# Two eight-product groups ahead of the seven-product bodies, and the up half of the gated unit left unscaled

## What is computed

```python
def rmsnorm(x, gain):
    xf = x.astype(jnp.float32)
    y = xf * lax.rsqrt(jnp.mean(xf * xf, axis=-1, keepdims=True) + EPS)
    return (y * gain.astype(jnp.float32)).astype(x.dtype)

def swiglu_2(x, w1, w3, w2):
    return (jax.nn.silu(x @ w1) * (x @ w3)) @ w2

    h = h + 0.5 * swiglu_2(rmsnorm(h, ffn1_norm[l]), ffn1_w1[l], ffn1_w3[l], ffn1_w2[l])
    ...
    h = h + 0.5 * swiglu_2(rmsnorm(h, ffn2_norm[l]), ffn2_w1[l], ffn2_w3[l], ffn2_w2[l])
```

## Time and profile before

| | |
|---|---|
| median of 3 runs | 1701.44 us (1700.73 to 1702.34) |
| the profiled execution | 1702.09 us |
| its span in the trace | 1700.3 us |
| instructions | 27271 |
| TensorE busy | 1585.5 us, 93% |
| VectorE busy | 1255.2 us, 74% |
| ScalarE busy | 755.0 us, 44% |
| GpSimd busy | 548.5 us, 32% |
| bytes moved | 187.26 MB, 110 GB/s in the mean |

### The profile page before, as it was taken

One profiled execution on the slowest core, in us unless ns is written; L12 is line 12 of the kernel. 1 busy time (PEld: TensorE's weight loads), 2 busy tenths in 40 slices (PEclk: granted clock), 3 DMA queues, 4 the chain that ended last, 5 costly groups with the idle time before them and its releaser, 6 DMA issues. The chain is left out here.

```text
span 1700.3 us, 27271 instructions
## 1 busy us (share of the span) xinstructions
PE 1585.5 (93%) x9945; PEld 1429.7 (84%) x9945; DVE 1255.2 (74%) x1542; ACT 755.0 (44%) x1267; POOL 548.5 (32%) x376
## 2 busy tenths in 40 slices
PE   9999999969999899969898989999998898897998
PEld 7888888859999888759888968888886798897887
DVE  5898665778999645799999874347455999998544
ACT  4553564435555634435545543221231555555322
POOL 0100000285666000175555302152038555551000
PEclk9999999979999999979999989999999899998999
DMA  9535502213343233213323222332212323232232
GB/s 389 202 111 176 188 29 75 75 62 124 123 139 120 71 103 98 101 62 124 123 99 121 77 75 93 118 137 100 75 53 72 122 101 117 100 116 68 91 96 81
DMA packets 34981, 187.26 MB, mean 110 GB/s; under 512 B 3680, under 2 KB 5984, under 8 KB 21472
## 3 DMA queue, kind: packets, MB, share of 16 engines
q1 hardware_dynamic: 30560, 169.53, 28.8%
q0 software_dynamic: 4352, 16.78, 2.8%
HBM read 184.20 MB, written 2.10 MB: 110 GB/s over the span
## 5 line engine op out<-in xcount | busy, mean ns | idle before, releaser
L663 PE MATMUL bank<-t_hi,ring 128*128 128x256 f32 x1920 | 366.5, 286 | 13.5 <-DVE ring L2565 11.2
L663 PE MATMUL bank<-g_hi,w_all 128*128 128x512 f32 (+1 forms) x1088 | 336.3, 391 | 20.3 <-DVE qd L2708 20.3
L2031 DVE TENSOR_TENSOR w_all<-w_raw,w_all 128x2048 fp32r<-128x2048 f32 x80 | 187.1, 2339 | 213.4 <-ACT w_all L1475 213.3
L663 PE MATMUL bank<-a_hi,ring 128*128 128x256 f32 x1440 | 283.1, 289 | 58.5 <-DVE tmp L2634 35.2
L663 PEld LDWEIGHTS bank<-t_hi,ring 128*128 128x128 f32 x1920 | 311.3, 195 | 14.1 <-DVE t_lo L2570 8.3
L663 PEld LDWEIGHTS bank<-a_hi,ring 128*128 128x128 f32 x1440 | 235.0, 195 | 66.9 <-DVE ring L2565 44.0
L1475 ACT ACTIVATE w_all<-w_raw 128x2048 fp32r<-128x2048 f32 x82 | 156.9, 1914 | 282.4 <-PE bank L663 282.4
L663 PE MATMUL bank<-t_lo,ring 128*128 128x256 f32 x960 | 274.6, 286 | 0.0
L663 PEld LDWEIGHTS bank<-g_hi,w_all 128*128 128x128 f32 x1088 | 206.6, 191 | 62.9 <-DVE qd L2708 20.9
L2565 DVE TENSOR_TENSOR ring<-w_sum,ring 128x512 fp32r<-128x512 f32 x240 | 240.8, 1021 | 23.9 <-ACT ring L1767 23.4
L663 PE MATMUL bank<-g_lo,w_all 128*128 128x512 f32 (+1 forms) x544 | 212.2, 390 | 0.0
(11 more groups left out here) (324 smaller groups left out, 2731.1 us busy)
## 6 DMA issues: line engine op xcount, KB each, us to landing
w_raw<-in_ffn_in SPq DMA_DIRECT2D x66, 1024.0 KB, 4.8
w_raw<-in_ffn_out SPq DMA_DIRECT2D x24, 768.0 KB, 4.3
mod_raw<-in_mod POOLq DMA_DIRECT2D x16, 1024.0 KB, 5.5
late<-in_ffn_in SPq DMA_DIRECT2D x30, 512.0 KB, 3.3
w_raw<-in_ffn_out SPq DMA_DIRECT2D x24, 640.0 KB, 3.9
w_raw<-in_gla_in SPq DMA_DIRECT2D x10, 1024.0 KB, 5.1
w_raw<-in_mix_in SPq DMA_DIRECT2D x10, 1024.0 KB, 4.8
mod_w<-in_mod SPq DMA_DIRECT2D x8, 1024.0 KB, 18.7
```

What stands on the lines that cost most here:

```text
L663: return pe.matmul(out, lhs, rhs, start=first, stop=last, skip_group_check=True)
L2031: V.tensor_tensor(flat(w_lo[s]), flat(w_raw[s]), flat(w_hi[s]).bitcast(F32), ALU.subtract).then_inc(lo_done[s], 1)
```

## The change

`BEFORE = 4` hidden chunks are now made by groups, two groups an FFN, and `BODIES` falls from ten to nine. The second group is a plain `group()`: gate unit, then up unit. SyncE loads four units ahead of the bodies' pairs, and `late` waits for four `up_ready`.

In `begin` of both engines the work is put in another order: the second group's two weight splits, the first group's SiLU and hidden chunks, then all four token operands, and only then the ring's first blocks, for they lie over the weights of the second group.

The up chunks are no longer multiplied by the roots. A hidden chunk is silu(gate x roots) x up, and since the roots are one number a token, the output chunks are multiplied by them instead, in PSUM, ahead of their sum (`sum_pair`, `add_half`): eight output chunks an FFN in place of 22 up chunks. Since the up banks are then free once `hid` is written, TensorE waits for `gated` there, not for `up_scaled`.

```diff
+BEFORE = 2 * CPU
+BODIES = (KF - BEFORE) // 2
...
@@ SyncE
-                for s in range(2):
-                    load(s, w_in[s])
+                for n in range(4):
+                    load(n % 2, w_in[n])
...
-                    sp.dma_start(flat(w_raw[s]), w_in[2 + s]).then_inc(pair_loaded[s], 16)
-                sp.wait_ge(up_ready, cnt.next(up_ready, CPU))
-                load_late(w_in[3, :, UNIT // 2:])
+                    sp.dma_start(flat(w_raw[s]), w_in[4 + s]).then_inc(pair_loaded[s], 16)
+                sp.wait_ge(up_ready, cnt.next(up_ready, BEFORE))
+                load_late(w_in[5, :, UNIT // 2:])
@@ TensorE
-                gate_free, up_free = (gate_scaled, up_scaled) if scaled else (silu_done, gated)
+                gate_free, up_free = gate_scaled if scaled else silu_done, gated
...
                 group(True)
+                group()
                 body(True)
@@ ScalarE, begin
+                    if not pair:
+                        split_hi(1)
+                    act.wait_ge(silu_in, cnt.next(silu_in, CPU) if scaled else CPU)
+                    split_hi(0)
+                    if not pair:
+                        copy_roots(5)
+                    gates(0)
+                    act.wait_ge(up_ready, cnt.next(up_ready, CPU))
+                    split_hi(1)
+                    token_upper(0)
+                    token_upper(1)
+                    token_upper(2)
+                    gates(CPU)
...
+                    token_upper(3)
+                    for j in range(4):
                         upper(j, True)
...
@@ VectorE, sum_pair
                     b = bank[banks[c]][:]
+                    if half:
+                        V.tensor_tensor(b, b, roots[:], ALU.mult).then_inc(up_scaled, 1)
+                        dve.wait_ge(up_scaled, cnt.next(up_scaled))
@@ VectorE, begin
+                def ups(m0):
+
+                    for c in range(CPU):
+                        dve.wait_ge(up_ready, cnt.next(up_ready))
+                        dve.wait_ge(silu_done, cnt.next(silu_done))
+                        V.tensor_tensor(hid[:, m0 + c], tmp[c][:], bank[2 + c][:], ALU.mult).then_inc(gated, 1)
+                        cnt.expect(gated)
@@ VectorE, hidden
-                    if scaled:
-                        V.tensor_tensor(tmp[2 + s][:], tmp[2 + s][:], roots[:], ALU.mult).then_inc(up_scaled, 1)
-                        dve.wait_ge(up_scaled, cnt.off(up_scaled, s - 1))
@@ VectorE, add_half
+                out = bank[6 + c][:] if half == 0 else bank[4 + c][:, h]
+                V.tensor_tensor(out, out, roots[:] if half == 0 else roots[:, h], ALU.mult).then_inc(up_scaled, 1)
+                dve.wait_ge(up_scaled, cnt.next(up_scaled))
```

More of the change, by code:

```diff
@@ L1267, in ffn @@
                 cnt.expect(operand_lo, 4)
-                cnt.expect(gate_free, KF - CPU)
-                if not scaled:
-                    cnt.expect(up_free, KF - CPU)
+                cnt.expect(gate_free, KF - BEFORE)
+                cnt.expect(up_free, KF - BEFORE)
                 for j in range(2):
@@ L2575, in hidden_lower, with gates @@
                     V.tensor_tensor(g_lo[:, k], hid[:, k], g_hi[:, k].bitcast(F32), ALU.subtract).then_inc(operand_lo, 1)
+                def gates(first=False):
+                    if not scaled:
+                        cnt.expect(silu_in, CPU)
+                        return
+                    for c in range(CPU):
+                        dve.wait_ge(silu_in, cnt.next(silu_in))
+                        if not first:
+                            dve.wait_ge(gated, cnt.now(gated, 1 - c))
+                        gate = bank[c][:]
+                        if first and pair and c == 0:
+                            dve.wait_ge(dve_step, cnt.now(dve_step))
+                            V.tensor_tensor(tmp[0][:], tmp[0][:], gate, ALU.add).then_inc(dve_step, 1)
+                            dve.wait_ge(dve_step, cnt.next(dve_step))
+                            gate = tmp[0][:]
+                        V.tensor_tensor(tmp[c][:], gate, roots[:], ALU.mult).then_inc(gate_scaled, 1)
+                        cnt.expect(gate_scaled)
+                def ups(m0):
+                    for c in range(CPU):
+                        dve.wait_ge(up_ready, cnt.next(up_ready))
+                        dve.wait_ge(silu_done, cnt.next(silu_done))
+                        V.tensor_tensor(hid[:, m0 + c], tmp[c][:], bank[2 + c][:], ALU.mult).then_inc(gated, 1)
+                        cnt.expect(gated)
                 def begin():
@@ L2586, in begin @@
                             split_lo(1)
-                            x_roots(5, False)
-                        for c in range(CPU):
-                            dve.wait_ge(silu_in, cnt.next(silu_in))
-                            gate = bank[c][:]
-                            if pair and c == 0:
-                                dve.wait_ge(dve_step, cnt.now(dve_step))
-                                V.tensor_tensor(tmp[0][:], tmp[0][:], gate, ALU.add).then_inc(dve_step, 1)
-                                dve.wait_ge(dve_step, cnt.next(dve_step))
-                                gate = tmp[0][:]
-                            V.tensor_tensor(tmp[c][:], gate, roots[:], ALU.mult).then_inc(gate_scaled, 1)
-                            cnt.expect(gate_scaled)
-                    else:
-                        cnt.expect(silu_in, CPU)
+                            x_roots(5)
+                    else:
+                        split_lo(0)
+                    gates(True)
+                    if scaled and pair:
+                        split_lo(0)
+                    ups(0)
+                    split_lo(1)
                     dve.wait_ge(joined, (KD + 2) * n + KD + 1)
                     V.tensor_tensor(t_sum[2][:], a_both[:, QK:KD, TC:T], a_both[:, 0:QK, TC:T], ALU.subtract).then_inc(t_late, 1)
-                    for j in range(3):
-                        lower(j)
                     token_lower(0)
@@ L2608, in begin @@
                     token_lower(1)
[L2609 to L2627 removed]
+                    token_lower(2)
+                    gates()
+                    token_lower(3)
+                    for j in range(4):
+                        lower(j)
+                    ups(CPU)
+                    lower(4)
                 def first_half(s):
```

55 lines of the change are left out of this document (13 added, 42 removed).

## The result

The changed kernel takes 1632.91 us (median of four runs, 1629.57 to 1635.18) against 1701.09 for the kernel before (four runs, 1699.36 to 1702.34). The ratio is 0.960, 95% interval 0.958 to 0.962. The profiled execution took 1632.69 us, its span is 1630.9. The forecast was 1626 us in a range of 1610 to 1641.

The account below looks back on a forecast made before the run. VectorE was taken to bound the bodies of FFN 1 and 2, TensorE those of FFN 0. The three FFN stretches fall from 719.6 to 643.8 us, 75.4 less with the tail: 1702.09 becomes 1626.7, forecast 1626, range 1610 to 1641.

Parts of the forecast that it names:

- Part 1: Each FFN: a second group of 21.8 us replaces a body of 20.1, +1.7 where TensorE is the bound.
- Part 2: Start of the bodies: the second group covers VectorE's work; gaps (15.1 us in FFN 0) shrink to about 0.5 a start.
- Part 3: Bodies of FFN 1 and 2: two root multiplications and waits go, 1.7 us; 23.03 becomes 21.3 us a body.
- rival B: Scaled bodies: VectorE falls below TensorE, bodies take 20.1 to 20.4 us, 1610 to 1617 in all; chance 0.18.
- Part 4: Gap before the output stage: 7.7 becomes 6.3 us in FFN 1 and 2; FFN 0 keeps 4.8.
- Part 5: Output chunks: eight multiplications an FFN, 0.7 us each, cost nothing inside; 0.45 us at FFN 2's last half chunk.
- the forecast's own case: Whole kernel: the time falls within 1618 to 1633 us; chance 0.55.
- C: Starts of the bodies still stall, 3 to 5 us each instead of 0.5; 1634 to 1640 us; chance 0.19.
- D: Scaled bodies stay at 23.03 us, set by the chain through gate multiplication and SiLU; 1650 us; chance 0.05.
- E: Scaled bodies: short waits grow past 2.3 us, bringing the low clock; 29.1 us a body, 1751 us; chance 0.02.

Follow-up runs that it names:

- the run with the early end: Changed kernel with the memsets that set `pair_out` ahead of the last ring blocks, and the last gate multiplications and hidden chunks later; 1624.74 us.
- the mended end: Changed kernel with early `pair_out`, FFN 2's inverse root earlier, two block sums on VectorE, and the second output weight split behind the sixth hidden chunk; 1588.60 us.
- the run with three sums moved: The run with the mended end, plus a third block sum (s2 of the second half) moved from GpSimd to VectorE; 1586.62 us.
- Four multiplications more: Changed kernel with 14 output chunks of FFN 1 and 2 multiplied by the roots five times instead of once; 1648.41 us.

## Why the prediction was right, and where it was off

**Part 1 (a group for a body)** held: the second group follows the first with no wait in FFN 0, and 327.86 to 371.83 is 44.0 us for two groups of 21.8.

**Part 2 (the cover)** held in FFN 1 and 2: no wait before the second body. In FFN 0 the first body waits 2.09 us for `first_half` where 0.5 was forecast and a gap over 2 us was named as a sign against. What was off is above all the mean price of a token operation. VectorE and GpSimd there:

```profile
355.55 1.23 DVE L2634 TENSOR_TENSOR t_sum<-a_both 128x1024 f32<-128x1024 f32 x1 [1.18 <-POOL a_both L572]
356.69 3.42 DVE L2582 TENSOR_TENSOR t_lo<-t_sum,t_hi 128x1024 fp32r<-128x1024 f32 x1
360.03 2.31 DVE L2637 TENSOR_TENSOR t_sum<-a_both,t_sum 128x1024 f32<-128x1024 f32 x1
362.27 6.79 DVE L2582 TENSOR_TENSOR t_lo<-t_sum,t_hi 128x1024 fp32r<-128x1024 f32 x3
```

```profile
355.60 3.43 POOL L581 TENSOR_TENSOR t_sum<-a_both,t_sum 128x1024 f32<-128x1024 f32 x1
```

The first token split took 3.42 us beside a token sum of GpSimd's of 3.43; the six operations took 13.4 us (355.55 to 368.98) instead of 10.6. In FFN 1 five of the six, with GpSimd idle, started 1.1 us apart (724.49 to 730.17). A mean over both was the wrong figure for either. Two smaller terms came on top in FFN 0: the four block splits behind them took 5.7 us (368.98 to 374.7) where 4.1 was counted, and VectorE stood 0.89 and 1.18 us, for ScalarE's split and for GpSimd's addition, where the sum had no wait at all. That GpSimd stretched the token operations is read from these rows; no run took its work away there.

**Part 3 (the bodies)** had the mechanism right and three sizes off. Forecast 21.3, measured 21.57, with TensorE's own turn at 20.16 and not 20.1: the forecast divided 80 us by 669 products, but such a count takes in the products that the edges of the stretch cut. The first multiplication and its wait gave back 0.83 (824.15 to 826.89 before, its like in the changed kernel 831.06 to 832.97), as counted. The second was counted at 0.6 and its wait at 0.24, and gave 0.60 in all: the two ring splits behind it went from 1.28 us to 2.38, since the sum that had fallen on the multiplication now fell on them, and filled the wait too. VectorE before, where the second `hidden` product's splits follow it, and around the first multiplication:

```profile
807.26 1.28 DVE L2565 TENSOR_TENSOR ring<-w_sum,ring 128x512 fp32r<-128x512 f32 x2
...
824.15 0.68 DVE L2654 TENSOR_TENSOR tmp<-tmp,roots 128x512 f32<-128x512 f32 x1
...
826.89 0.41 DVE L2634 TENSOR_TENSOR tmp<-qd,bank 128x256 f32<-128x256 f32 x1
```

That the delay passes on, not away, is what told this forecast from rival B; the two sums that were taken away or moved showed that it is a delay of GpSimd's making. The third size is the lead of the first body: I let seven of nine bodies pay 1.2 us, 8.4; FFN 1 paid 10.9 (742.08 to 940.71, less 9 x 20.16 and 6.3) and FFN 2 11.3, which is some eight bodies at 1.41. The 8.0 us that were missed are then 0.5 in each FFN for TensorE's own turn, 2.0 and 2.4 in FFN 1 and 2 beyond the 8.9 that were forecast for bodies and start, and 2.0 in FFN 0 for its wait with the loss around it.

**Part 4 (the ends)**: 6.28 and 4.83 us against 6.3 and 4.8. The forecast took the chain for needed; the run with the early end showed that it isn't. In FFN 1 of the changed kernel the last VectorE operation that reads bank 5 is the second `first_half` of the last body, at 921.98 (0.41 us), and the output stage starts at 940.71.

**Part 5 (the output chunks)**: no wait inside the output stages; FFN 1's has the same length (121.7 us, from its first to its last product), and FFN 2's stage with all behind it is 133.2 us against 132.9, 0.3 for the forecast's 0.45. The last half chunk's multiplication starts at 1620.87 and its sum at 1621.34, 0.47 us later.

**The cases.** The time fell into the forecast's own case, but only just (1618 to 1633): without the 2.1 us that went where nobody edited it would have been above it, within the range all the same. B asked for bodies at 20.1, C for 3 to 5 us a start, D for 23.03, E for longer short waits; none stands in the trace. A gap did cost more than its length, as E had it: with the mended end no wait stands before the output stage of FFN 1, and that stage takes 119.6 us instead of 121.7, some 2 us less (1.9 in FFN 2; 2.8 in FFN 0, whose stage also differs by 1.2 us between the two kernels). But E's 2.3 us is no limit that holds: behind three waits of 3.01 us each the clock was 1.00, 0.50 and 0.68.

## What to carry to other kernels

When an engine is the bound, count what its neighbour does to it: a sum that GpSimd made "for free" cost VectorE 1.1 us, more than the 0.61 of making it itself. Price an operation beside GpSimd and one without it apart, never by their mean. And a wait that stood in both kernels, such as the one before the output stage, should be asked what it guards: here it guarded banks whose last reader had finished 17 to 18 us before.

## What was not expected of the hardware

- A GpSimd operation of one column takes 0.57 us where VectorE's takes 0.16, and its sum of 128 x 512 takes 1.29 us when it goes first, where VectorE's operations of that shape start 0.61 apart.
- The length of a wait alone doesn't decide TensorE's clock behind it. After 2.09 us in FFN 0 of the changed kernel the next product took 0.39, at the high clock; in the run with three sums moved, after 2.06 us at the same place it took 0.58, at the low one. Longer waits of equal length differ too: see the three of 3.01 us under "Four multiplications more". The row of the run with three sums moved:

```profile
379.29 0.58 PE L670 MATMUL bank<-a_hi,ring 128*128 128x256 f32 x1 [2.06 <-DVE tmp L2674]
```
